# Overflow branch in the middle of the experts, embedding projection between down slabs, eleven weight slots

## The reference

```python
for i in range(2):
    h = rms_norm(x, norm_mix[i])
    q, k, v, cu, cg, ga, gb = split(h @ w_in[i])          # 1024 -> 4608
    y_a = dilated_mixture_attention(rope(q), rope(k), v) @ w_attn_out[i]
    y_b = conformer_conv(cu, cg, ...) @ w_conv_out[i] + b_conv_out[i]
    x = x + (sigmoid(ga) * y_a + sigmoid(gb) * y_b) @ w_out[i]
    h2 = rms_norm(x, norm_ffn[i])
    # 32 experts in 4 groups: the best group, in it the best 2 experts of each token
    x = x + sum(gate[e] * ((silu(h2 @ w_gate[e]) * (h2 @ w_up[e])) @ w_down[e]))
    g = sigmoid(rms_norm(x, norm_ple[i]) @ w_ple_gate[i])  # 1024 -> 1024
    x = x + g * (p[i] @ w_ple_proj[i])                     # 256 -> 1024
x = rms_norm(x, norm_final)
```

## Time and profile before

| | us |
|---|---|
| median of 3 runs (lowest, highest) | 2069.28 (2068.17, 2074.96) |
| the profiled execution | 2068.92 |
| its span, first to last instruction | 2066.8 |
| TensorE matmuls busy | 1727.0 (84%) |
| VectorE, ScalarE busy | 545.8, 335.2 |
| moved by DMA | 560.97 MB, mean 271 GB/s |

### The profile page before, as it was taken

How to read it: one execution, slowest core, us unless ns; L and a number is a source line. 1 busy time by engine, 2 the same in 40 slices (tenths; PEclk the granted TensorE clock), 3 DMA queues, 4 the chain that set the end, 5 groups by cost and what they waited for, 6 DMA issues and landing times. The chain is left out here.

```text
span 2066.8 us, 21051 instructions
## 1 busy us (share of the span) xinstructions
PE 1727.0 (84%) x9170; PEld 1120.7 (54%) x9170; DVE 545.8 (26%) x1109; ACT 335.2 (16%) x695; POOL 0.2 (0%) x4
## 2 busy tenths in 40 slices
PE   7999967666665899998666576679999999999999
PEld 6788522212221787883222122147888877888744
DVE  3853200000000376431000000025566333210000
ACT  2231200000000222310000000012152244210000
POOL 0000000000000000000000000000000000000000
PEclk9999987888888999999888878889999999999999
DMA  8436699999999634359999999981433333333441
GB/s 341 163 133 248 279 427 428 427 429 426 429 427 428 256 131 155 134 233 408 427 428 426 428 428 428 428 344 70 157 132 137 125 109 95 122 142 143 163 162 62
DMA packets 40175, 560.97 MB, mean 271 GB/s; under 512 B 4464, under 2 KB 4464, under 8 KB 5744
## 3 DMA queue, kind: packets, MB, share of 16 engines
q1 hardware_dynamic: 40080, 559.57, 66.7%
HBM read 558.50 MB, written 1.05 MB: 271 GB/s over the span
## 5 line engine op out<-in xcount | busy, mean ns | idle before, releaser
L1182 PE MATMUL ps<-ring,hB 128*32 128x512 f32 x1344 | 196.0, 712 | 119.7 <-DMA ring<-in_stream 119.7
L1574 PE MATMUL ps<-hA,ring 128*128 128x256 f32 (+1 forms) x1312 | 289.2, 382 | 0.6 <-DVE b_sc L2202 0.6
L1574 PEld LDWEIGHTS ps<-hA,ring 128*128 128x128 f32 (+1 forms) x1312 | 246.4, 188 | 42.2 <-issue 4.6
L563 PE MATMUL ps<-hA,ring 128*128 128x256 f32 x1152 | 253.0, 380 | 0.0
L563 PEld LDWEIGHTS ps<-hA,ring 128*128 128x128 f32 x1152 | 217.7, 190 | 32.7 <-issue 3.7
L1182 PEld LDWEIGHTS ps<-ring,hB 128*32 128x32 f32 x1344 | 41.7, 121 | 271.3 <-DMA ring<-in_stream 135.8
L1182 PE MATMUL ps<-l_extra,hB 128*32 128x512 f32 x704 | 117.5, 802 | 82.5 <-DMA l_extra<-in_stream 82.5
L1193 PE MATMUL ps<-ring,l_work 128*32 128x512 f32 x704 | 106.0, 736 | 55.7 <-DMA ring<-in_stream 47.2
L1274 DVE TENSOR_TENSOR l_work<-ps,l_work 128x512 f32<-128x512 f32 x16 | 11.1, 692 | 436.5 <-ACT l_work L1248 436.5
L1182 PEld LDWEIGHTS ps<-l_extra,hB 128*32 128x32 f32 x704 | 23.0, 128 | 163.5 <-DMA l_extra<-in_stream 93.4
L1836 PE MATMUL ps<-ring 128*128 128x512 f32 x256 | 110.0, 592 | 0.0
(11 more groups left out here) (317 smaller groups left out, 1696.3 us busy)
## 6 DMA issues: line engine op xcount, KB each, us to landing
ring<-in_stream SPq DMA_DIRECT2D x189, 2048.0 KB, 37.6
l_extra<-in_stream SPq DMA_DIRECT2D x64, 2048.0 KB, 40.8
ring<-in_stream SPq DMA_DIRECT2D x6, 1792.0 KB, 16.6
ring<-in_stream SPq DMA_DIRECT2D x4, 1344.0 KB, 7.9
ring<-in_stream SPq DMA_DIRECT2D x2, 1764.0 KB, 9.0
ring<-in_stream SPq DMA_DIRECT2D x2, 1024.0 KB, 29.8
b_bias<-in_bias SPq DMA_DIRECT2D x1, 2048.0 KB, 12.9
xT<-in_xT SPq DMA_DIRECT2D x1, 1024.0 KB, 4.8
```

What stands on the lines that cost most here:

```text
L563: mm = self.nc.tensor.matmul(out[:, m * T:(m + 1) * T], w[:, k, c * P:(c + 1) * P], src[:, k, :], start=(k == 0), stop=(k == kc - 1))
L1182: mm = nc.tensor.matmul(out[js, :], x_slots[q % 2][:, c, js], w[:, 0, j * D + n0:j * D + n0 + FF], start=(c == 0), stop=(c == DC - 1))
L1574: mm = nc.tensor.matmul(out[0:width, m * T:(m + 1) * T], w[:, k, (c0 + m) * width:(c0 + m + 1) * width], src[:, k, :], start=(k == 0), sto ...
```

## The change

- The branch moves to the middle of the experts. A block now holds the second four quads of the layer before, its embedding part, the dense part, and the first four quads of its own layer. `layer_block` and `ple_block` become `block`, which runs three times. At the middle, SyncE stops issuing two slots short of what is free, and `over_block` uses these two slots (one for the weights, one for its input and sum).
- The slots for experts' slabs become eleven: `l_extra` gets a fourth slot that holds no activations and stands first in `cycle`, and a slot `late`, last in `cycle`, in which hA and the tiles raw and sig lie in the dense part. The first slab of a layer in `late` is issued only after the transposes of `htok` (a wait of SyncE on filled["htok"]).
- Room for it: the reserve for software descriptors is cut to 1024 bytes, `work` to 4096 columns, and some parameters of the second block are loaded later; `x_slots` is single, `y_slots` lies in hB, silu is written in place, kn and vn of the second block lie in `late`.
- The slab of w_ple_proj comes before the last quad's four down slabs, and the four banks of the projection are done ahead of and between them. `ple_tensor` is then only the gate and the mean; the additions of the last quad alternate with the gains.

```diff
-RING, EXTRA = 6, 3
+RING, EXTRA = 6, 4
+LATE = RING + EXTRA
+CYCLE = LATE + 1
+SPLIT = QUADS // 2
+MOE_SLABS = QUADS * QUAD_SLABS
 SLAB = 4096
...
+    def expert(self, layer, m):
+
+        return self.first[layer, "moe"] + m + (m >= MOE_SLABS - FC)
...
-        cycle = cycle[:3] + [RING + 1, cycle[3], RING + 2, RING] + cycle[4:]
+        cycle = [RING + 3] + cycle[:3] + [RING + 1, cycle[3], RING + 2, RING] + cycle[4:] + [LATE]
         guard = {RING + 1: s.first[l, "y_a"], RING + 2: s.first[l, "y_b"], RING: s.first[l, "w_out"]}
         s.last.update(guard)
-        for m in range(QUADS * QUAD_SLABS):
-            s.add((l, "moe"), [cycle[m % len(cycle)]], P, 1, SLAB)
+        for m in range(MOE_SLABS):
+            if m == MOE_SLABS - FC:
+                s.add((l, "ple"), [cycle[m % CYCLE]], P, PLE // P, D, m0 + MOE_SLABS)
+            s.add((l, "moe"), [cycle[(m + (m >= MOE_SLABS - FC)) % CYCLE]], P, 1, SLAB, m0 + m)
         tail = ring if l < DEPTH - 1 else range(3, RING)
-        s.add((l, "ple"), tail, P, PLE // P, D)
         for _ in range(2):
             s.add((l, "ple_gate"), tail, P, DC, BANK)
     for _ in range(3):
...
             if before is not None and before >= self.known:
                 sp.wait_ge(*self.freed[before])
-            sp.dma_start(self.slot(s)[0:rows, 0:chunks * cols], self.stream[i, 0:rows, 0:chunks * cols]).then_inc(self.landed[s], 16)
+            if i in self.guard:
+                sp.wait_ge(*self.guard[i])
+            sp.dma_start(self.slot(s)[0:rows, 0:chunks * cols], self.stream[self.slabs.at[i], 0:rows, 0:chunks * cols]).then_inc(self.landed[s], 16)
             self.issued += 1
 
...
-        work = sb("work", [P, 5632])
+        work = sb("work", [P, 4096])
...
-        self.raw = work[:, 0:1024].rearrange(three, c=2)
-        self.sig = work[:, 1024:2048].rearrange(three, c=2)
...
+        self.raw = store.late[:, 2048:3072].rearrange(three, c=2)
+        self.sig = store.late[:, 3072:4096].rearrange(three, c=2)
...
+        self.x_slots = flat_b[:, 0:DC * P].rearrange(three, c=DC)
+        self.y_slots = flat_b[:, DC * P:2 * DC * P]
...
-        for stage, bs in dict(ple=(0, 1, 2, 3), mean_ple=(7,), ple_gate=(4, 5, 6, 7),
+        for stage, bs in dict(ple=(0, 1, 4, 5), mean_ple=(7,), ple_gate=(2, 3, 6, 7),
...
     def ple_tensor(self, pe, claim, layer):
-        first = self.store.slabs.first
-        self.project(pe, claim, first[layer, "ple"], "ple", 0, self.pT)
+        first, store = self.store.slabs.first, self.store
+        i = first[layer, "ple_gate"]
+        w = store.wait(pe, i)
+        self.fill_bank(pe, claim, "ple_gate", 0, w, 0, self.hA, DC, self.scaled["ple"])
         self.mean_square(pe, claim, "ple")
-        for n in range(2):
-            self.project(pe, claim, first[layer, "ple_gate"] + n, "ple_gate", 2 * n, self.hA, self.scaled["ple"] if n == 0 else None)
+        self.fill_bank(pe, claim, "ple_gate", 1, w, 1, self.hA, DC)
+        store.free(i, self.filled["ple_gate"], 2)
+        self.project(pe, claim, i + 1, "ple_gate", 2, self.hA)
 
     def ple_scalar(self, act, step, then_norm):
...
     def ple_scalar(self, act, step, then_norm):
         for b in range(4):
+            act.wait_ge(self.part_added, 4 * (QUADS - SPLIT - 1) + b + 1)
             self.square_bank("ple", b)
...
-        self.scale_by_gain(layer, "ple", range(DC))
+        added = 4 * (QUADS - SPLIT - 1)
+        for b in range(5):
+            if b < 4:
+                self.add_part(dve, added + b)
+            if b:
+                dve.wait_ge(self.part_added, added + b)
+                self.scale_by_gain(layer, "ple", range(2 * b - 2, 2 * b))
         for b in range(4):
...
+            if q == QUADS - 1:
+                i = store.slabs.first[layer, "ple"]
+                w = store.wait(pe, i)
+                self.fill_bank(pe, claim, "ple", 0, w, 0, self.pT, PLE // P)
+            pe.wait_ge(self.hidT_ready, n + 1)
+            if n:
+                pe.wait_ge(self.y_left, n)
+                pe.wait_ge(self.y_right, n)
             for f in range(FC):
-                down(q, f)
-        combine(QUADS - 1)
-
-    def moe_scalar(self, act):
+                down(q, n, f)
+                if q == QUADS - 1 and f < FC - 1:
+                    if f == 1:
+                        pe.wait_ge(self.put_copied, n + 1)
+                    self.fill_bank(pe, claim, "ple", f + 1, w, f + 1, self.pT, PLE // P)
+                    if f == FC - 2:
+                        store.free(i, self.filled["ple"], 4)
+        combine(n)
+
+    def moe_scalar(self, act, q0, q1, n0):
...
+            nc.scalar.activation(self.hid_slots, ps[0][:], ACT.Silu).then_inc(self.gu_silu, 1)
...
+    def block(self, layer, inputs):
+
+        store, slabs = self.store, self.store.slabs
+        head, tail = layer < DEPTH, layer > 0
+        n0 = QUADS - SPLIT if tail else 0
         with self.nc.Block(no_gpsimd_drain=True) as block:
 
             @block.tensor
             def _(pe):
                 claim = self.claimer(pe)
-                if layer:
+                if tail:
                     inputs.wait_p(pe, layer - 1)
+                    self.moe_tensor(pe, layer - 1, SPLIT, QUADS, 0, claim)
                     self.ple_tensor(pe, claim, layer - 1)
                 else:
                     inputs.wait(pe)
-                self.front_tensor(pe, claim, layer)
-                self.moe_tensor(pe, layer)
+                if head:
+                    self.front_tensor(pe, claim, layer)
...
             @block.sync
             def _(sp):
-                if layer == 0:
+                if not tail:
                     inputs.first(sp)
                     store.issue(sp, 2)
                     inputs.rest(sp)
+                if head:
+                    if tail:
+                        store.issue(sp, slabs.until(slabs.first[layer, "q"] - 1))
+                        sp.wait_ge(self.filled["ple"], 4)
+                    inputs.load_p(sp, layer)
+                    m0 = slabs.first[layer, "moe"]
+                    store.guard[next(i for i in range(m0, len(slabs.slot)) if slabs.slot[i] == LATE)] = (self.filled["htok"], 4)
+                    half = slabs.expert(layer, SPLIT * QUAD_SLABS)
+                    store.issue(sp, min(slabs.until(half - 1), half + CYCLE - 2))
                 else:
-                    store.issue(sp, store.slabs.until(first[layer, "q"] - 1))
-                    sp.wait_ge(self.filled["ple"], 4)
-                inputs.load_p(sp, layer)
-                store.issue(sp, store.slabs.until(first[layer, "moe"] + QUADS * QUAD_SLABS - 1))
+                    store.issue(sp, slabs.until(slabs.first["u_rnn"] - 1))
         store.next_block()
 
 
     def over_block(self, layer):
...
-        keep = dict(xT=sb("xT", [P, DC, T]), hA=sb("hA", [P, DC, T]), hB=sb("hB", [P, DC, T]), const=sb("const", [P, C_COLS]))
+        late = sb("late", [P, SLAB])
+        keep = dict(xT=sb("xT", [P, DC, T]), hA=late[:, 0:DC * T].rearrange("p (c n) -> p c n", c=DC), late=late, hB=sb("hB", [P, DC, T]), const=sb("const", [P, C_COLS]))
...
-    nc = _bacc.Bacc("TRN2", target_bir_lowering=False, num_devices=1)
+    nc = _bacc.Bacc("TRN2", target_bir_lowering=False, num_devices=1, dynamic_dma_scratch_size=1024)
```

More of the change, by code:

```diff
@@ L213, in __init__, with add @@
     def __init__(self):
-        self.slot, self.before, self.nth, self.shape, self.name = [], [], [], [], []
-        self.last = {s: None for s in range(RING + EXTRA)}
-        self.count = {s: 0 for s in range(RING + EXTRA)}
+        self.slot, self.before, self.nth, self.shape, self.at = [], [], [], [], []
+        self.last = {s: None for s in range(CYCLE)}
+        self.count = {s: 0 for s in range(CYCLE)}
         self.first = {}
-    def add(self, name, slots, rows, chunks, cols):
+    def add(self, name, slots, rows, chunks, cols, at=None):
         s = min(slots, key=lambda k: -1 if self.last[k] is None else self.last[k])
@@ L370, in __init__ @@
         self.extra = None
-        self.landed = [ctx.enter_context(nc.semaphore(f"landed{i}")) for i in range(RING + EXTRA)]
-        self.freed = []
+        self.late = late
+        self.guard = {}
+        self.landed = [ctx.enter_context(nc.semaphore(f"landed{i}")) for i in range(CYCLE)]
+        self.freed = {}
         self.issued = 0
@@ L1277, in moe_vector @@
-        add_parts(QUADS - 1)
-    def layer_block(self, layer, inputs):
-        store, first = self.store, self.store.slabs.first
+        if q0:
+            self.choose(dve, q0, n0)
+            self.choose_gate(dve, q0, n0)
+        for q in range(q0, q1):
+            n = n0 + q - q0
+            if q < q1 - 1:
+                self.choose(dve, q + 1, n + 1)
+                self.choose_gate(dve, q + 1, n + 1)
+            if q > q0:
+                for b in range(4):
+                    self.add_part(dve, 4 * (n - 1) + b)
+            dve.wait_ge(self.gu_silu, n + 1)
```

(14 more changed lines are left out.)

329 lines of the change are left out of this document (154 added, 175 removed).

## The result

The changed kernel takes 2023.74 us (median of four runs, 2022.89 to 2026.88) against 2069.24 for the kernel before on the same chips: ratio 0.9777, 95% interval 0.9757 to 0.9798. That is 45.5 us less; 48 were forecast, and the time lies inside the range. The execution that the profile shows is the longest of the four, 2026.88, with a span of 2025.1; against the profiled execution of before it is 42.0 us shorter.

What follows compares the result with a forecast made beforehand. TensorE bounds the dense parts, DMA the experts, then a passage back to TensorE. Terms -19.8 - 33.8 + 4.9 = -48.7 us against 2068.92 gave 2020.2; with median offset and half a microsecond, 2021, range 2015 to 2032.

Steps and rivals of the forecast that it cites:

- Two more slots: Ahead of each layer's experts: eleven slabs instead of nine loaded or under way, -9.9 us per layer, -19.8 in all.
- The passage: Last down slab to next dense matmul: only combine stands before ple_gate; -16.8 us in layer 0, -17.0 in layer 1.
- Half a slab ahead of the last four: End of each layer's experts: the projection's weights (1024 KB) load before the last four down slabs, +2.5 us per layer, +4.9.
- The sum of these for the expert stretches: Expert stretch of each layer: two slots' -9.9 us and the half slab's +2.5 together, -7.4 per layer.
- The branch: Mid-experts: TensorE idles but queued slabs keep DMA busy, cost 0; without that cover up to 19.5 us per layer.
- Rival 1: Extra expert slots: only one slab per layer is won, 2031 us, chance 0.10; or none, 2041, chance 0.04.
- Rival 2: At the branch: the code fetch waits behind the full DMA queue, about 5 us per layer, 2031; chance 0.07.
- Rival 4: Expert loading: a deeper queue lowers the transfer rate, slower than before; at 5.3 us per slab 2082 us; chance 0.03.
- Rival 3: Passage at half clock: down slabs +1.9, then first ple_gate bank up to +3.5 us per layer, 2025 to 2032; chance 0.14.
- (e): The rest (buffer placement, smaller bpar, larger late, overflow block not run, layout of work): 0, bounds -1 to +2 us.
- a sign of error: Second block: the prediction is wrong if the span from its first matmul to the end, about 648 us, changes.

Runs made afterwards that it cites:

- nine_slots: The changed kernel with only the nine expert slots of the kernel before (neither hA's slot nor the one holding no activations): median 2044.1 us.
- L0: Not a run: the moment of layer 0's last down slab's first matmul, read off each kernel's timeline.
- projection_after: The changed kernel with the embedding projection undone: its slab after the last down slab, its four banks between combine and the gate: median 2034.43 us.
- E0: Not a run: the moment of layer 0's first expert matmul, read off each kernel's timeline; E0 to L0 took 433.69 us before, 427.11 changed.

## Why the prediction was right, point by point

- **Two more slots: -19.8 forecast, -19.7 measured** (nine_slots). The time of a slab from the earlier trace rows and the gap in the earlier trace rows were the right two readings (427 GB/s make 4.91 us for a slab rather than 4.94, 0.1 us per layer). The slab in hA's slot went out at 220.54, forecast 220.75.
- **The passage: -16.8 and -17.0 forecast, -17.2 and -17.3 measured.** The gate began 6.65 us behind L0 (6.9), q 35.1 (35.5). The reciprocal ended 16.9 us behind it (17.2) and held nothing up.
- **Half a slab ahead of the last four: +2.5 forecast, 2.1 and 2.3 measured** in projection_after.
- **The sum of these for the expert stretches** was -7.4 per layer and came out at -6.6 and -6.2. nine_slots is 3.3 and 3.7 us above before where 2.2 is the half slab. Some 1.2 us per layer are left over. One kernel's stretches repeat within 0.8. A later branch (split_at_seven) leaves the stretches as they are and a second one (two_branches) adds 1.1 and 0.3, but no run has these stretches without a branch. The DMA packets say more: from E0 to L0 they carry 87.53 slabs' worth of weights in the kernel before, so 86.03 were due, and 86.14 to 86.30 came in the three profiles of the changed kernel, at 4.91 us each in both kernels. So most of the 1.2 us is 0.1 to 0.3 of a slab more to load within the stretch, 0.5 to 1.3 us, and not a stop of the transfers; why a little more is left to load is open.
- **The branch: 0 forecast; no cost shown** (a second one leaves the median among those of the changed kernel), and 12 to 14 per layer once the queue is taken away, where I had put the uncovered price at up to 19.5. That bound took TensorE's stop; the DMA's, which decides, ends at SyncE's first issue, 8 us behind the last down's end and not 18.
- **Rival 1** fell with nine_slots. **Rival 2** was right that code is fetched ahead of TensorE's restart, and wrong on the wait behind the queue and on the price. **Rival 4**: the rate is 427 GB/s with eleven slots as with nine. **Rival 3** is the interesting one: it never came at the last down slab with the projection's banks ahead of it, it did come at four of the slabs ahead of that one in the changed kernel's three profiles, off the path or nearly, and in the two kernels without the banks it was real (3.49 and 3.42 us). And the lower clock came where I had not looked.
- **What was missed: +2.7 us of 2021 against 2023.7.** The step that failed is (e) together with the second half of rival 3: I took the second block's 648 us as fixed because its instructions are, and named a change of it only as a sign of error. That sign came: it took 646 to 653, by the clock. In the profile this is 5.6 of the 6.7 us by which -42.0 falls short of -48.7. The 1.1 that are left are the stretches, 2.1 short together, less the passages' 0.7 and some 0.4 in small differences elsewhere. That the median fell only 2.7 us short is luck in part: the dip is in all three profiles of the changed kernel, in one of them only in part, and how many of the unprofiled executions had it isn't known.

## What to carry to other kernels

A barrier and a branch cost nothing here once they stand where the DMA is the limit and has its work queued. When you move one to such a place, count the queue against the right stop: the stop of the engine that issues the transfers (8 us here) has to be covered, not that of the engine that computes. Ahead of a stretch limited by DMA a free buffer was worth one transfer (4.8 to 5.0 us, once 5.9), so buffers that hold something only in the dense part are worth giving back at the last reader. Work put between the pieces of a stretch that waits for DMA paid twice, once off the path, and once because the piece that ends the stretch then had a short wait ahead of it and ran at full clock. And instructions that don't change need not take the same time: the clock alone moved one block by 7 us.

## What the runs showed of the hardware that I had not expected

- TensorE's pause behind a branch ended 1.5 to 1.8 us behind a 16 KB packet of the instruction queue in all 25 pauses of 5.6 us or more. It was 5.7 us with nothing in the DMA queue, and with seven to nine transfers of 2 MB queued 8.3 to 8.8 in layer 0 and 2.7 to 8.6 in layer 1.
- A slab's 16 matmuls behind a wait took 1.92 us or up to 3.6, the longer ones at the lower clock. With a 2 us bank of other matmuls in each gap eight of 88 were slow, all behind waits of 2.05 us or more, and the last one, with a wait of 1.06 at most, never.
- The clock also falls inside unbroken work of TensorE, among very small matmuls, in some executions and not in others, for the same instructions: 646.1 to 653.2 us.
